# Three matrix loads of the expert loop, each cut into transfers of 112, 8 and 8 partitions

## The chip, the cores and the metric

The kernel runs on one core of one Trainium2 chip. The metric is the device time of one execution in microseconds (us). Three runs of the kernel before gave 1307.75, 1304.37 and 1307.27 us, so the median is 1307.27 us. All arithmetic is in float32.

## The reference, cut to what matters

One inference step of a one-layer decoder for 256 prompt tokens and 32 sample tokens (8 requests of 4 tokens): RWKV-7 time mixing and a convolution module side by side, cross-attention over memory tokens, then a mixture of 32 experts of which each token takes 4. The change touches only the mixture of experts:

```python
for e in range(N_EXPERTS):                       # 32 experts, D_MODEL = D_EXPERT = 1024
    gate = jnp.minimum(t @ w_gate[e] + b_gate[e], SWIGLU_LIMIT)
    up = jnp.clip(t @ w_up[e] + b_up[e], -SWIGLU_LIMIT, SWIGLU_LIMIT)
    hid = (up + 1.0) * gate * jax.nn.sigmoid(gate * SWIGLU_ALPHA)
    y = y + comb[:, e:e + 1] * (hid @ w_down[e] + b_down[e]).astype(jnp.float32)
```

Each expert has three matrices of 1024 x 1024 float32, which is 4 MB each. All 96 matrices are read from HBM once, some 403 MB.

## The kernel before, in words

The first 340 us or so compute the mixing, the convolution and the attention. The rest is the expert loop: 16 pairs of experts, numbered 0 to 15. For each pair TensorE multiplies by six matrices in this order: first gate, first up, second gate, second up, first down, second down (`MATRICES`). Each product is 32 matmuls of `L1182`. Between them stand the transposes of the hidden rows (`L1199`, `L1207`), the gathering of the next pair's token rows (`L1211`), the bias rows (`L1193`) and the addition of the last pair's result to the output (`L1244`, `L1256`).

The matrices wait in ten slots of SBUF, each 128 partitions of 16 KB, six in the tensor `ring` and four in `arena`. In pairs 2 to 14 (`WHOLE`) a matrix goes as one transfer into two neighbouring slots: 128 rows of 32 KB, one row to each partition (`L465`). So five matrices fit at a time. In pairs 0, 1 and 15 a matrix goes as two halves of 2 MB or as smaller pieces (`L487`, `L485`, `L481`).

All these loads are issued by SyncE in program order. Before a load, SyncE waits (`wait_used`) until TensorE has finished the product that read what was in the slots, which is the matrix five places earlier. The load then stands in the DMA queue behind those issued before it. When a load has landed it adds 16 to the semaphore of its slot (`slot_in[i]`), and TensorE waits before the first matmul of a product until the semaphore stands at 16 times the number of loads that the slot has had (`landings`, used in `product`).

Ahead of pair 0's second gate matrix, `small()` (`L441`) loads three bias tables of 128 KB: each is 32 rows of 4 KB, to partitions 0 to 31, 32 to 63 and 64 to 95.

Of the kernel before, what the change touches and what calls it, by code (L numbers as in the profile page):

```python
# [21 lines left out]
P = 128  # L22
# [14 lines left out]
SLOTS = 10  # L37
TURN = (2, 3, 4, 5, 6, 7, 8, 9, 0, 1)
WHOLE = range(2, PAIRS - 1)
BIASED = 6  # L40
RING = 6
RW = 14
CT = 4
# [36 lines left out]
LOADS = 12 * PAIRS  # L80


def load_of(q, n, c):

    return 12 * q + 2 * n + c


def slot_of(load):

    return TURN[load % SLOTS]  # L90


def asked(load):

    return load | 1 if load // 12 in WHOLE else load


def landings(load):

    i = slot_of(load)  # L100
    return len({asked(l) for l in range(load + 1) if slot_of(asked(l)) == i})


PER_ROUND = [len({asked(l) for l in range(LOADS) if slot_of(asked(l)) == i}) for i in range(SLOTS)]
OPENED = 6


# [42 lines left out]
def build(nc, A, O):  # L150
    with ExitStack() as ctx:
        def sb(name, shape, dt=F32):
            return ctx.enter_context(nc.sbuf_tensor(name, shape, dt))

        def sem(name):
            return ctx.enter_context(nc.semaphore(name))

        def part(base, at, *dims):

            n = 1  # L160
            for d in dims:
                n *= d
            a = base[:, at:at + n]
            names = "abcd"[:len(dims)]
            if len(dims) == 1:
                return a
            return a.rearrange(f"p ({' '.join(names)}) -> p {' '.join(names)}", **dict(zip(names, dims)))

        SLOT = 4 * D
        SPARE = 27096 - (SLOTS - 8) * SLOT  # L170
        ring = sb("ring", [P, RING * SLOT])
        scratch = ring[:, 2 * SLOT:]
# [3 lines left out]
        vec = sb("vec", [P, VECW])  # L176
        slot = [part(ring, i * SLOT, KT, 512) for i in range(RING)]

        def weights(i):

            if i < RING:
                return ring[:, i * SLOT:(i + 1) * SLOT]
            at = (i - RING) * SLOT if i < 8 else SPARE + (i - 8) * SLOT
            return arena[:, at:at + SLOT]

        def whole_slot(i):

            if i < RING:
                return ring[:, (i - 1) * SLOT:(i + 1) * SLOT]
            at = 0 if i < 8 else SPARE  # L190
            return arena[:, at:at + 2 * SLOT]
# [89 lines left out]
        load = const[:, 1221:1222]  # L281
# [71 lines left out]
        slot_in = [sem(f"slot_in{i}") for i in range(SLOTS)]  # L353
# [26 lines left out]
        def _(sp):  # L380
# [58 lines left out]
            def small():  # L439
                for dst, name in ((b_gate, "b_gate"), (b_up, "b_up"), (b_down, "b_down")):  # L440
                    sp.dma_start(dst, A[name]).then_inc(S["ext_ld"], 16)  # L441
# [7 lines left out]
            def wait_used(r, load):  # L449

                q, n, c = load // 12, load % 12 // 2, load % 2
                if frees(n, c):
                    sp.wait_ge(S["used"], r * (USED * PAIRS) + used_up_to(load))
                else:
                    sp.wait_ge(S["up_done" if n in (1, 3) else "down_done"], r * (2 * PAIRS) + (2 * q + 1 + (n in (3, 5))))

            def experts(r, q):
                opening, last = isinstance(r, int) and q == 0, q == PAIRS - 1
                for n, (w, p) in enumerate(MATRICES):
                    e = 2 * q + p  # L460
                    if q in WHOLE:
                        load = load_of(q, n, 1)
                        i = slot_of(load)
                        wait_used(r, load - SLOTS)
                        sp.dma_start(whole_slot(i), w[e, :, :]).then_inc(slot_in[i], 16)  # L465
                        continue
                    for c in range(2):
                        load = load_of(q, n, c)
                        i = slot_of(load)
                        src = w[e, :, c * SLOT:(c + 1) * SLOT]  # L470
                        if load < SLOTS:
                            if opening and i < len(last_front):
                                name, val = last_front[i]
                                sp.wait_ge(S[name], val)
                        elif not (opening and n == 5):
                            wait_used(r, load - SLOTS)
                        if opening and i == RING:
                            small()
                        if last and n == 5:
                            for k in range(4):  # L480
                                sp.dma_start(weights(i)[:, k * D:(k + 1) * D], src[:, k * D:(k + 1) * D]).then_inc(S[LAST_ROWS[c][k]] if k < 3 else slot_in[i], 16)  # L481
                        elif opening and n == 5:
                            for k in range(4):
                                sp.wait_ge(S["used"], 4 * c + k + 1)
                                sp.dma_start(weights(i)[:, k * D:(k + 1) * D], src[:, k * D:(k + 1) * D]).then_inc(S["x_in"] if k < 3 else slot_in[i], 16)  # L485
                        else:
                            sp.dma_start(weights(i), src).then_inc(slot_in[i], 16)  # L487
# [9 lines left out]
            for q in range(PAIRS):  # L497
                experts(0, q)
# [4 lines left out]
            with sp.Fori(1, ROUNDS) as r:  # L503
                with sp.If(n > r * CAP):
                    for q in range(PAIRS):
                        experts(r, q)
                    final_rows(r)
                    results(r)
                    sp.wait_ge(S["out_sent"], r * (16 * PARTS) + 16 * PARTS)
                    sp.sem_inc(S["router_in"], 1)  # L510
# [85 lines left out]
        def _(pe):  # L596
# [569 lines left out]
            def product(out, lhs, r, q, n, ks, fresh, done=None, swap=False):  # L1166

                opening, pieces, whole = isinstance(r, int) and q == 0, q == PAIRS - 1 and n == 5, q in WHOLE
                for k in ks:
                    load = load_of(q, n, k // 4)  # L1170
                    i = slot_of(load)
                    if pieces and k % 4 < 3:
                        pe.wait_ge(S[LAST_ROWS[k // 4][k % 4]], r * 16 + (48 if k == 2 else 32))
                    elif whole and k == 0 or not whole and k % 4 == 0 or pieces and k % 4 == 3:
                        come = slot_of(asked(load))
                        pe.wait_ge(slot_in[come], r * (16 * PER_ROUND[come]) + 16 * (FRONT_FILLS[come] + landings(asked(load))))
                    if opening and n == 0 and k == 4:
                        pe.wait_ge(S["xe_ready"], 2)
                    if opening and n == 5 and k == 0:
                        pe.wait_ge(S["x_in"], 16 + 6 * 16)  # L1180
                    for h in range(2):
                        last = nc.tensor.matmul(out[AT[h ^ swap], :], lhs(k), part(weights(i), 0, 4, D)[:, k % 4, h * 512:(h + 1) * 512],  # L1182
                                                start=(fresh and k == 0), stop=(k == KT - 1), skip_group_check=True)
                    if opening and n == 0 or k % 4 == 3 and frees(n, k // 4):
                        last.then_inc(S["used"], 1)
                if done and k == KT - 1:
                    last.then_inc(S[done], 1)
# [74 lines left out]
            def step(r, q, s):  # L1262
# [11 lines left out]
                opening = isinstance(s, int) and first  # L1274
                biased = isinstance(s, int) and q == BIASED
                half, rest = range(KT // 2), range(KT // 2, KT)
# [949 lines left out]
```

## Time and profile before

| | |
|---|---|
| median of 3 runs | 1307.27 us |
| the profiled execution | 1306.09 us |
| its span, first to last instruction | 1304.3 us |
| TensorE busy | 1265.9 us (97%) |
| VectorE, ScalarE busy | 412.6 us, 192.3 us |
| moved by DMA | 464.67 MB, 356 GB/s over the span |
| granted TensorE clock, mean | 0.993 |

The span is the time between the first and the last instruction of the profiled execution; 1.8 us of the execution lie outside it. A busy TensorE is read from modelled ends of matmuls. The DMA share of a stretch is the part of it in which the core's 16 DMA engines, on average, had a packet under way: 1.00 is all sixteen all the time. GB/s is what arrived meanwhile. The two together tell whether the engines are idle or slow.

### The profile page before, as it was taken

What the parts mean: (1) busy time and instruction counts of PE and PEld (TensorE: products, weight loads), DVE (VectorE), ACT (ScalarE), POOL (GpSimd) and SP (SyncE); (2) the same over time, 40 slices, a digit from 0 to 9 for tenths busy, and PEclk for the clock granted to TensorE, in tenths of its full rate; (3) what the DMA queues carried; (4) which work ended last, traced back from release to release, by engine and by line L of the source; (5) the groups of instructions that cost most, each with busy time, mean ns of one, the idle gap of its engine ahead of it and who ended that gap; (6) DMA issues with size and microseconds to landing.
All of it is one profiled execution on the core that took longest, in us unless ns stands there. A gap on an engine that the chain in (4) does not pass through costs nothing.

```text
span 1304.3 us, 18542 instructions
## 1 busy us (share of the span) xinstructions
PE 1265.9 (97%) x8160; PEld 623.3 (48%) x8160; DVE 412.6 (32%) x836; ACT 192.3 (15%) x353; POOL 11.7 (1%) x31
## 2 busy tenths in 40 slices
PE   9999999999999999999999999999999999999995
PEld 7777865677763443434434343443334343343332
DVE  4987745433122122131222212122121212212122
ACT  4114322221121010000100000010000001010002
POOL 0001000000000000000000000000000000000000
PEclk9999999999999999999999999999999999999998
DMA  9333041495999999999999999999999999999993
GB/s 319 131 107 141 4 140 60 164 379 227 414 409 426 427 433 432 433 428 432 432 431 431 428 431 433 433 433 426 430 431 433 434 431 431 428 430 433 425 424 143
DMA packets 30335, 464.67 MB, mean 356 GB/s; under 512 B 7329, under 2 KB 8865, under 8 KB 12465
## 3 DMA queue, kind: packets, MB, share of 16 engines
q1 hardware_dynamic: 29600, 459.53, 83.9%
q0 software_dynamic: 656, 3.96, 0.7%
q8 instruction: 66, 1.08, 0.3%
q14 instruction: 13, 0.10, 0.0%
HBM read 458.34 MB, written 5.14 MB: 355 GB/s over the span
## 4 chain that ended last, share of the span: by engine, by line
PE 78%; DMA 18%; DVE 1%; ACT 1%; issue 0%; SPq 0%; DVEq 0%
PE ps L1182 39%; PE ps L605 25%; DMA ring<-in_w_down 9%; DMA arena<-in_w_down 9%; PE ps L1211 5%; PE ps L1256 3%; PE ps L1193 2%; PE ps L1207 1%; PE ps L1199 1%; PE ps L1304 1%; DVE ring L1602 0%; DMA ring<-in_w_in 0%; PE ps L1244 0%; PE ps L1258 0%; DVE arena L1605 0%
## 5 line engine op out<-in xcount | busy, mean ns | idle before, releaser
L1182 PE MATMUL ps<-ring,xT 128*64 128x512 f32 x1216 | 270.8, 595 | 0.7 <-DMA ring<-in_w_up 0.6
L605 PE MATMUL ps<-arena,ring 128*128 128x288 f32 (+3 forms) x1136 | 225.4, 366 | 1.4 <-DMA ring<-in_w_in 1.3
L605 PEld LDWEIGHTS ps<-arena,ring 128*128 128x128 f32 (+1 forms) x1136 | 176.7, 177 | 47.7 <-issue 4.7
L1182 PE MATMUL ps<-arena,xT 128*64 128x512 f32 x832 | 185.5, 595 | 0.1
L1357 ACT ACTIVATE arena<-ps 128x512 f32<-128x512 f32 (+5 forms) x136 | 76.4, 570 | 630.2 <-PE ps L1199 363.2
L1182 PEld LDWEIGHTS ps<-ring,xT 128*64 128x64 f32 x1216 | 83.9, 137 | 176.6 <-issue 173.2
L1182 PE MATMUL ps<-ring,arena 128*64 128x512 f32 x640 | 145.1, 601 | 8.0 <-DMA ring<-in_w_down 8.0
L1182 PEld LDWEIGHTS ps<-arena,xT 128*64 128x64 f32 x832 | 57.4, 137 | 120.3 <-issue 117.6
L1182 PE MATMUL ps<-arena 128*64 128x512 f32 x384 | 87.6, 604 | 7.6 <-DMA arena<-in_w_down 7.6
L1182 PEld LDWEIGHTS ps<-ring,arena 128*64 128x64 f32 x640 | 45.2, 138 | 92.7 <-issue 91.6
L2065 DVE TENSOR_TENSOR arena<-arena,ps 128x512 f32<-128x512 f32 x64 | 44.0, 687 | 130.2 <-PE ps L1256 117.3
L2017 DVE TENSOR_TENSOR xT<-ps,vec 128x1024 f32<-128x1024 f32 x15 | 18.4, 1224 | 173.6 <-PE ps L1211 173.6
L1256 PE MATMUL ps<-arena 128*128 128x512 f32 x128 | 63.8, 619 | 0.0
L1211 PE MATMUL ps<-arena 128*128 128x128 f32 x512 | 62.8, 282 | 0.0
L1211 PEld LDWEIGHTS ps<-arena 128*128 128x128 f32 x512 | 59.8, 196 | 2.0 <-issue 0.2
L2075 DVE TENSOR_SCALAR xT<-ps 128x512 f32<-128x512 f32 x32 | 22.1, 691 | 121.1 <-PE ps L1193 121.1
L605 PE MATMUL ps<-ring,arena 128*32 128x256 f32 (+4 forms) x456 | 59.1, 382 | 0.8 <-ACT arena L1357 0.8
L1182 PEld LDWEIGHTS ps<-arena 128*64 128x64 f32 x384 | 27.2, 139 | 58.6 <-issue 57.9
L1551 ACT ACTIVATE xT<-xT 128x512 f32<-128x512 f32 x32 | 20.1, 630 | 237.1 <-DVE xT L2075 237.1
L1605 DVE SCALAR_TENSOR_TENSOR arena<-arena,vec 128x256 f32<-128x256 f32 x128 | 51.5, 481 | 2.5 <-ACT arena L1370 2.5
L2080 DVE TENSOR_SCALAR xT<-ps 128x512 f32<-128x512 f32 x32 | 22.0, 687 | 81.7 <-PE ps L1182 81.7
L2105 DVE COPY arena<-ps 64x512 f32<-64x512 f32 x16 | 10.9, 683 | 99.3 <-PE ps L1182 99.3
(227 smaller groups left out, 765.6 us busy)
## 6 DMA issues: line engine op xcount, KB each, us to landing
ring<-in_w_gate SPq DMA_DIRECT2D x16, 4096.0 KB, 34.8
ring<-in_w_up SPq DMA_DIRECT2D x16, 4096.0 KB, 35.1
ring<-in_w_down SPq DMA_DIRECT2D x14, 4096.0 KB, 36.9
arena<-in_w_down SPq DMA_DIRECT2D x12, 4096.0 KB, 35.0
arena<-in_w_gate SPq DMA_DIRECT2D x10, 4096.0 KB, 32.6
arena<-in_w_up SPq DMA_DIRECT2D x10, 4096.0 KB, 35.4
ring<-in_w_down SPq DMA_DIRECT2D x8, 2048.0 KB, 19.7
ring<-in_w_gate SPq DMA_DIRECT2D x6, 2048.0 KB, 17.6
```

The source lines that it names most:

```text
L605: return nc.tensor.matmul(out, lhsT, rhs, start=start, stop=stop)
L1182: last = nc.tensor.matmul(out[AT[h ^ swap], :], lhs(k), part(weights(i), 0, 4, D)[:, k % 4, h * 512:(h + 1) * 512], start=(fresh and k == ...
L1193: last = nc.tensor.matmul(out[AT[h], :], one_e[o, p, :], b[:, h * 512:(h + 1) * 512], start=(out is psU), stop=(out is psG), skip_group_ch ...
L1211: last = nc.tensor.matmul(to[:, k * P:(k + 1) * P], h_tok[:, j, k * P:(k + 1) * P], pick[:, j, :, :], start=False, stop=(j == 1), skip_gro ...
L1256: last = nc.tensor.matmul(out, gT[:, h, j * P:(j + 1) * P], ye[h], start=True, stop=not biased, skip_group_check=True)
L1357: return a.activation(out, in_, ACT.Copy, scale=scale)
L1551: nc.scalar.activation(sig, gmin, ACT.Sigmoid, scale=1.702).then_inc(S["sig_ready"], 1)
L1605: return v.scalar_tensor_tensor(out, x, s, y, o0, o1)
L2017: nc.vector.tensor_tensor(xe.rearrange("p k a c -> p k (a c)"), psX.rearrange("p (k t) -> p k t", k=KT), g_moe.unsqueeze(2).broadcast_to([ ...
L2065: nc.vector.tensor_tensor(y[:, j, at], y[:, j, at], (psY, psX)[j][:, at], ALU.add).then_inc(S["y_added"], 1)
L2075: nc.vector.tensor_scalar(gmin, psG, 7.0, None, ALU.min).then_inc(S["g_ready"], 1)
L2080: link(nc.vector.tensor_scalar(ug, psU, 7.0, -7.0, ALU.min, ALU.max))
```

## The change

The first gate matrix of pairs 3, 7 and 11 is no longer one transfer of 128 partitions but three, issued one behind the other: partitions 0 to 111, 112 to 119 and 120 to 127. They go to the same two slots, read the same rows of HBM and add to the same semaphore, 48 in place of 16. Loads are now counted by transfers, so that TensorE's wait for this product and for later ones of that slot ask for the higher count. Nothing else is computed or loaded otherwise.

```diff
+UNEVEN = (3, 7, 11)
+SHARES = (slice(0, 112), slice(112, 120), slice(120, 128))
...
+def shares(load):
+
+    return SHARES if load // 12 in UNEVEN and load % 12 < 2 else (slice(0, P),)
+
+
+def transfers(i, loads):
+
+    return sum(len(shares(load)) for load in {asked(l) for l in loads} if slot_of(load) == i)
+
+
 def landings(load):
 
-    i = slot_of(load)
-    return len({asked(l) for l in range(load + 1) if slot_of(asked(l)) == i})
-
-
-PER_ROUND = [len({asked(l) for l in range(LOADS) if slot_of(asked(l)) == i}) for i in range(SLOTS)]
+    return transfers(slot_of(load), range(load + 1))
+
+
+PER_ROUND = [transfers(i, range(LOADS)) for i in range(SLOTS)]
...
-                        sp.dma_start(whole_slot(i), w[e, :, :]).then_inc(slot_in[i], 16)
+                        for rows in shares(load):
+                            sp.dma_start(whole_slot(i)[rows], w[e, rows, :]).then_inc(slot_in[i], 16)
```

SyncE's queue before, from the last loads of pair 2 to the first of pair 3:

```order
L465 DMA ring<-in_w_down 128x8192 [waits down_done]
L453 REGISTER_ALU
L465 DMA arena<-in_w_down 128x8192 [waits used]
L455 REGISTER_ALU
L465 DMA arena<-in_w_gate 128x8192 [waits up_done]
L453 REGISTER_ALU
L465 DMA ring<-in_w_up 128x8192 [waits used]
L455 REGISTER_ALU
L465 DMA ring<-in_w_gate 128x8192 [waits up_done]
```

The same place now:

```order
L477 DMA ring<-in_w_down 128x8192 [waits down_done]
L464 REGISTER_ALU
L477 DMA arena<-in_w_down 128x8192 [waits used]
L466 REGISTER_ALU
L477 DMA arena<-in_w_gate 112x8192 [waits up_done]
L477 DMA arena<-in_w_gate 8x8192 x2
L464 REGISTER_ALU
L477 DMA ring<-in_w_up 128x8192 [waits used]
L466 REGISTER_ALU
L477 DMA ring<-in_w_gate 128x8192 [waits up_done]
```

The load of the first gate matrix is 112 partitions wide and is followed by two of 8 partitions, with no wait of their own; everything else keeps its place. Pairs 7 and 11 change in the same way. On TensorE, VectorE, ScalarE and GpSimd no operation is added, removed or moved; only numbers that TensorE and SyncE wait for are others.

## Rows read from the trace of the kernel before

**Rows 1.** The page: engines' busy time, DMA share by slices, instruction fetches.
```profile
PE 1265.9 (97%) x8160; PEld 623.3 (48%) x8160; DVE 412.6 (32%) x836; ACT 192.3 (15%) x353; POOL 11.7 (1%) x31
...
DMA  9333041495999999999999999999999999999993
...
q8 instruction: 66, 1.08, 0.3%
```

**Rows 2.** Windows, pairs 2 to 14: busy us, clock, DMA share, GB/s.
```profile
core 0: us, PE busy (x) PEld busy (x) DVE busy (x) ACT busy (x) POOL busy (x), PEclk, DMA share, GB/s
455.00:1215.00 760.00, 743.70 (x3819) 284.83 (x3817) 169.25 (x314) 65.34 (x107) 0.00 (x0) 1.00 1.00 431
```

**Rows 3.** DMA queues, same stretch: packets, MB, share of 16 engines.
```profile
q1 hardware_dynamic: 11270, 326.98, 100.1%
q8 instruction: 30, 0.49, 0.3%
```

**Rows 4.** Who TensorE waited for: us in total, times, longest.
```profile
PE ps L1182 <- DMA ring<-in_w_down: 8.0, 3, 2.7
PE ps L1182 <- DMA arena<-in_w_down: 7.6, 3, 2.7
...
PEld ps L1182 <- DMA ring<-in_w_up: 3.3, 3, 1.5
PEld ps L1182 <- DMA arena<-in_w_up: 2.7, 3, 0.9
```

**Rows 5.** Chain of waits, pairs 9 to 10: start us, us, what.
```profile
883.79 38.19 DMA arena<-in_w_down
...
922.12 3.65 PE ps L1182 x16
...
941.86 38.41 DMA ring<-in_w_down
...
980.40 3.65 PE ps L1182 x16
```

**Rows 6.** Chain of waits, pair 14 to the end.
```profile
1176.55 38.40 DMA arena<-in_w_down
...
1215.09 5.03 PE ps L1182 x16
...
1275.93 10.48 PE ps L1182 x47
```

**Rows 7.** Windows at the end of the last weight load.
```profile
1274.00:1276.00 2.00, 2.00 (x14) 0.73 (x12) 0.17 (x1) 0.04 (x1) 0.00 (x0) 1.00 1.02 401
1276.00:1278.00 2.00, 2.00 (x10) 0.63 (x10) 0.00 (x0) 1.97 (x3) 0.00 (x0) 1.00 0.63 231
1278.00:1280.00 2.00, 2.00 (x12) 0.72 (x10) 0.00 (x0) 0.52 (x2) 0.00 (x0) 1.00 0.51 209
...
1282.00:1284.00 2.00, 2.00 (x12) 0.64 (x10) 0.00 (x0) 0.00 (x0) 0.00 (x0) 1.00 0.49 195
```

**Rows 8.** Windows around the landing of the bias tables.
```profile
354.00:356.00 2.00, 2.00 (x10) 1.58 (x9) 0.46 (x1) 0.11 (x1) 0.00 (x0) 1.00 1.02 434
356.00:358.00 2.00, 2.00 (x14) 0.99 (x14) 0.45 (x1) 0.44 (x1) 0.00 (x0) 1.00 1.13 275
358.00:360.00 2.00, 2.00 (x10) 1.56 (x9) 0.46 (x1) 0.00 (x0) 0.00 (x0) 1.00 0.95 256
360.00:362.00 2.00, 2.00 (x10) 1.54 (x9) 0.24 (x1) 0.00 (x0) 0.00 (x0) 1.00 1.03 330
362.00:364.00 2.00, 2.00 (x10) 1.58 (x9) 0.67 (x2) 0.44 (x1) 0.00 (x0) 1.00 0.96 410
```

**Rows 9.** DMA issues between 334 and 336 us: KB, us to landing.
```profile
arena<-in_b_gate SPq DMA_DIRECT2D x1, 128.0 KB, 24.1
...
arena<-in_b_down SPq DMA_DIRECT2D x1, 128.0 KB, 27.3
```

**Rows 10.** Windows while 512 KB pieces of 128 partitions land (4 KB rows).
```profile
391.00:397.00 6.00, 6.00 (x48) 2.50 (x42) 0.94 (x3) 2.30 (x3) 0.00 (x0) 1.00 1.02 408
```

**Rows 11.** Timeline of SyncE's queue, then of TensorE, around pair 3's first gate matrix.
```profile
509.45 0.33 SPq L465 DMA_DIRECT2D arena<-in_w_gate  x1
519.77 0.33 SPq L465 DMA_DIRECT2D ring<-in_w_up  x1
...
547.08 7.04 PE L1182 MATMUL ps<-arena,xT 128*64 128x512 f32 x32
```

## The prediction

> **What bounds the kernel now.** I read the page first. TensorE is busy for 1265.9 us, 97% of the span, and the DMA engines are busy in every slice from about a quarter of the span on [rows 1]. Two resources are nearly full, so the averages don't tell which one sets the end.
>
> The windows do. Over pairs 2 to 14 the DMA share is 1.00 and 431 GB/s arrive, while TensorE is idle for 760 - 743.7 = 16.3 us [rows 2]. A matrix of 4.19 MB takes 4.19 MB / 431 GB/s = 9.73 us, and six take 58.4 us. The chain of waits shows the same period: the wait that ends at 922.12 us comes again at 980.40, 58.3 us later [rows 5]. TensorE needs less for a pair: 58.3 less the 2.7 us that it waited for a down matrix and some tenths for an up matrix, about 55 us. So the DMA engines are the slower of the two throughout. In the early pairs this doesn't show, because the five slots hold matrices ahead; the gate matrix that is issued at 509.45 us is only needed at 547.08, 37.6 us later [rows 11]. From pair 9 on the stock is used up, and TensorE waits six times for a down matrix, 15.6 us together, and 6.0 us for up matrices [rows 4]. What the queues lose before that is not forgiven: since they never rest, a loss at pair 3 is still there at pair 10.
>
> The last such wait ends at 1215.09 us [rows 6]. From there TensorE runs almost without a gap to the end, so the kernel's end moves with the landing of pair 14's first down matrix, one for one.
>
> The third view is the end of the stream. Up to 1276 us all sixteen engines work; from 1278 to 1284 the share is 0.51 to 0.49 and about 209 GB/s arrive [rows 7]. Eight engines had finished and eight were still at it, 8 us late. A load has landed only when its last engine has, so TensorE always waits for the late eight. Why they are late: there were 66 instruction fetches, 0.3% of sixteen engines' 1304 us [rows 1], which is 0.003 x 16 x 1304 = 63 us. If they all fall on eight engines, that is 7.8 us for each, and the 8 us are explained.
>
> **The change part by part.** *Rows moved.* The queue moved 326.98 MB in 11270 packets, 29 KB each with the few small ones [rows 3], so a 32 KB row goes as one packet on one engine, and an engine takes 9.73 / 8 = 1.22 us for it. 112 rows are 7 for each of 16 engines. Eight rows can be spread over eight engines at most, and if both small transfers use the same eight, these get 9 rows and the others 7. Three times this is 3.65 us more for one half and 3.65 us less for the other. If the early half gets the extra rows, it ends at 1276 + 3.65 = 1279.7 and the late half at 1284 - 3.65 = 1280.3: nearly even. With nothing else, the end comes 3.65 us earlier.
>
> No row shows which engines a small transfer takes. The Trainium skill ("DMA: Bandwidth & Descriptors", Why a DMA increments its semaphore by 16 and not by 1) says that a transfer uses the largest number up to 16 that divides its slowest dimension, and on this queue the lowest-numbered engines: 16 for 112 rows, the first eight for 8 rows.
>
> *Issues.* Six more DMA issues at 0.33 us each [rows 11] are 2.0 us of SyncE, at places where it has 8 to 10 us until its next wait ends (509.45 to 519.77). They cost nothing while the queue holds matrices, and at most 0.7 us a place if it didn't. TensorE's waits are the same in number.
>
> *Narrow targets.* This term decides. The trace has narrow transfers at one place: three bias tables of 32 partitions, 393 KB together, that land between 358 and 363 us (issued between 334 and 336, 24.1 to 27.3 us to landing) [rows 9]. There the rate falls from 434 to 275, 256, 330 and 410 GB/s while the DMA share stays about 1 [rows 8]. The engines were not idle; their packets took longer. Against 431 GB/s this is (156 + 175 + 101 + 21) x 2 us = 906 KB not moved, 2.1 us of the whole stream. It isn't the small rows: pieces of the same 4 KB rows, but over 128 partitions, go at 408 GB/s [rows 10], which would cost 0.1 us here. So writes that aim at few partitions hold each other up, and others' too.
>
> The new transfers aim at 8 partitions, 262 KB each. Bounds for the two of one matrix, 524 KB: nothing, if eight engines on eight partitions don't meet; at the bias tables' price per byte 2.1 x 524 / 393 = 2.8 us. If the price grows as the target narrows, 32 / 8 = four times this, 11.2 us. The dear end: sixteen engines fill 128 partitions at 431 GB/s, 26.9 GB/s for 8 partitions; if 8 neighbours have no more than that, the two transfers take 19.5 us in place of 2 x 1.22, 17.1 us more. I take 9.7 us: it is between 2.8 and 17.1 and near the scaled value, which is the only one that uses both the measured loss and the width. It falls on the eight engines that carry the small transfers.
>
> The skill states a rule that speaks against the change ("SBUF — State Buffer", Door 1: The DMA port swizzle): SBUF has 16 DMA ports of 27.2 GB/s, and groups of four neighbouring partitions share one, so 8 neighbours reach two ports. It gives 27.6 GB/s measured on partitions 0 to 3. By it the two small transfers take 2 x 262 KB / 54.4 GB/s = 9.6 us, an estimate, and 12 us with the other half's own rows on these ports; that is 7.2 to 9.6 us over the free price. The trace agrees in kind [rows 8] and has no 8-partition write to measure.
>
> *Sum.* The half with the small transfers loses 1.22 + 9.7 = 10.9 us a matrix, 32.8 us over three. It was 8.0 us ahead, so the last landing comes 24.8 us later. The other half gains 3.65 us, which helps nothing. Nothing hides the loss: the stock of five slots was going to be empty at pair 9 anyway, and now is empty some pairs sooner. 1306.09 + 24.8 = 1330.9 us. The profiled run is 1.2 us below the median of the three, within their spread, so I say 1331.
>
> **The rivals.** *Balance.* The narrow writes cost nothing, and the late half does less: 1306.1 - 3.65 = 1302.4 us, or 1303.6 against the median. For it: eight engines are late by 8 us [rows 7], and 3.65 us each way meets that closely. Against it: rows 8. It decides if the narrow term is below (8.0 - 3.65) / 3 = 1.4 us a matrix.
>
> *Light price.* The bias price per byte, 2.8 us for every engine or 5.6 us on one half: 3 x (1.22 + 2.8 or 5.6) - 8.0 = 4.1 to 12.5 us, 1310 to 1319. For it: it is the measured figure as it stands.
>
> *The wide part collides too.* In one transfer of 128, eight rows belong to each engine and nothing collides (431 GB/s). Seven rows for each may put several engines on the same partitions' path. If that holds up half to all of their 8.5 us, another 4.3 to 8.5 us a matrix, 13 to 26 us: 1344 to 1357. No row shows a transfer of 112.
>
> *Wrong half.* The extra rows go to the engines that are already late: with no narrow price 1306.1 + 3.65 = 1309.7, with it 1306.1 + 32.8 = 1339. The rows can't tell the halves apart.
>
> *Nothing.* If the small transfers are spread over all engines after all, the time stays at 1306 to 1307.
>
> **How the numbers follow.** Forecast, narrow price near 9.7 us, 1322 to 1340: 0.52. Balance 0.17. Light price 0.10. Wide part collides 0.14. Wrong half without a narrow price 0.04. Nothing 0.03. The range of 1302 to 1346 holds balance, and leaves out most of the dear case. This kernel's measurement tells 0.3% from no change, 3.9 us. Balance lies just at this bound, so half of it, 0.09, counts as faster; its other half with nothing and a third of the wrong half, 0.12, as the same; the rest, 0.79, as slower.
>
> **What would show it.** Right: in windows of 2 us after about 525, 760 and 1000 us GB/s falls well below 400 for 8 to 15 us while the DMA share stays near 1; the mean over pairs 2 to 14 falls from 431 to about 417 GB/s; TensorE's first wait for a down matrix comes two to four pairs sooner, and its waits for DMA grow from 21.6 to about 46 us; the gate loads' time to landing grows. Balance: no dips, the windows after 1276 us fall from full share to nothing within 2 us, and the waits shrink by 3.65 us. Light price: dips as at 356 us and no deeper. A dip that begins with the 112-row part is the third rival. I am wrong if no dip stands at these three places.

## The result, and the profile after

The changed kernel takes 1369.43 us (median of 6 runs, 1363.79 to 1374.04); the kernel before took 1305.53 us in the same comparison. The ratio is 1.0484, 95% interval 1.0456 to 1.0512: 63 us slower, give or take 4. The forecast was slower by 24.8 us, 1331, with a range up to 1346. The direction was right and the size was not. The profile below is of the execution that took 1363.79 us, the fastest of the six and 57.7 us above the profiled one of before.

The page of the changed kernel, its engines and its DMA by slices:

```profile
span 1362.0 us, 18548 instructions
...
PE 1280.5 (94%) x8160; PEld 629.4 (46%) x8160; DVE 412.8 (30%) x836; ACT 192.2 (14%) x353; POOL 11.7 (1%) x31
...
DMA  8342052478999999999999999999999999999993
GB/s 307 124 152 86 3 187 98 172 295 356 403 410 429 433 429 255 432 429 432 430 430 432 309 332 430 429 431 431 431 383 209 424 431 433 431 431 430 427 418 115
```

The DMA share is as full as in [rows 1], but three dips stand in GB/s: 255, then 309 and 332, then 383 and 209. They are where the cut matrices of pairs 3, 7 and 11 land. Between them the rate is the 431 GB/s of [rows 2]. The windows of the changed kernel (columns as in [rows 2]), first the whole stretch, then the three dips, then the first dip in two parts:

```profile
455.00:1240.00 785.00, 726.53 (x3668) 279.78 (x3666) 159.08 (x295) 62.83 (x103) 0.00 (x0) 0.97 1.00 402
520.00:550.00 30.00, 30.00 (x172) 12.67 (x168) 6.58 (x14) 3.00 (x5) 0.00 (x0) 1.00 0.98 243
765.00:800.00 35.00, 17.66 (x98) 9.00 (x98) 2.11 (x4) 2.30 (x4) 0.00 (x0) 0.77 1.00 226
1010.00:1065.00 55.00, 30.55 (x142) 12.96 (x140) 4.19 (x7) 2.37 (x4) 0.00 (x0) 0.78 1.00 259
...
500.00:516.00 16.00, 16.00 (x76) 4.99 (x72) 5.86 (x9) 0.63 (x1) 0.00 (x0) 1.00 1.01 435
518.00:532.00 14.00, 14.00 (x70) 4.43 (x68) 4.46 (x10) 1.04 (x2) 0.00 (x0) 1.00 0.98 234
532.00:542.00 10.00, 10.00 (x74) 6.29 (x72) 0.16 (x1) 1.78 (x3) 0.00 (x0) 1.00 1.03 144
545.00:560.00 15.00, 15.00 (x74) 4.71 (x72) 3.37 (x7) 0.61 (x2) 0.00 (x0) 1.00 0.99 425
```

Time lost in a stretch is its length times the missing share of 431 GB/s. Over the whole stretch that is 785 x (1 - 402/431) = 52.8 us. The dips give 30 x (1 - 243/431) = 13.1, 16.6 and 22.0 us, 51.7 together: the whole loss is in them, and it grows from one to the next. (The first dip begins 2 us ahead of its window, which adds 0.9 us.) In the first dip the 112-row part comes first, 14 us at 234 GB/s, a loss of 6.4 us; then come the 8-row parts, 10 us at 144 GB/s, a loss of 6.7 us.

The DMA queue of the changed kernel at 480 to 510 us, where nothing is cut, then in the two parts of the first dip (packets, MB, share of 16 engines):

```profile
q1 hardware_dynamic: 442, 12.91, 100.0%
q1 hardware_dynamic: 109, 3.28, 98.4%
q1 hardware_dynamic: 72, 1.44, 103.1%
```

A packet is one row of 32 KB, apart from those of 4 bytes. By the MB these are 394 rows, then 100, then 44, and they share the time of sixteen engines: 1.22 us a row, then 2.2, then 3.75. The packets' own records say that no engine was spared. From 518 to 531.5 us no row took less than 1.69 us, and from 534 to 540 none of 27 less than 3.63. At least 11 of the 27 belong to other transfers, since the two small ones have 16 rows in all.

Who TensorE waited for in the changed kernel (total us, times, longest), to be read beside [rows 4]:

```profile
PE ps L1194 <- DMA ring<-in_w_down: 19.2, 7, 7.0
PE ps L1194 <- DMA ring<-in_w_gate: 15.7, 2, 14.5
PE ps L1194 <- DMA arena<-in_w_gate: 14.4, 1, 14.4
PE ps L1194 <- DMA arena<-in_w_down: 10.0, 5, 2.7
```

59.3 us in place of 15.6, with two waits of over 14 us. The 14.4 us are a wait for a cut matrix, the first gate matrix of pair 7: the timeline has its end in the third row. In the course of the wait the granted clock falls from 1.00 to 0.50, and it stays there for the first 5 us or so of the work behind it (0.77 and 0.78 in the dips' means).

```profile
769.50 3.84 PE L1223 MATMUL ps<-arena 128*128 128x128 f32 x32
776.23 8.78 PE L1194 MATMUL ps<-ring,arena 128*64 128x512 f32 x32 [2.90 <-DMA ring<-in_w_down]
799.46 2.83 PE L1194 MATMUL ps<-arena,xT 128*64 128x512 f32 x6 [14.44 <-DMA arena<-in_w_gate]
```

With 5.6 us for which the weight loads of TensorE's array (PEld) waited, its waits for DMA are 65 us, where the forecast had about 46. The first wait for a down matrix ends at 642 us, in pair 4, five pairs sooner than before.

The end of the stream, which answers to [rows 7]:

```profile
1334.00:1336.00 2.00, 2.00 (x10) 0.57 (x8) 0.00 (x0) 1.97 (x3) 0.00 (x0) 1.00 0.28 100
...
1338.00:1340.00 2.00, 2.00 (x12) 0.71 (x10) 0.00 (x0) 0.69 (x2) 0.00 (x0) 1.00 0.13 52
...
1342.00:1344.00 2.00, 2.00 (x12) 0.48 (x8) 0.00 (x0) 0.00 (x0) 0.00 (x0) 1.00 0.06 25
```

Before, eight engines were late together. Now the stage at half share is gone: up to 1334 us the share is about 0.9, then 0.13 is two engines and 0.06 is one. So the two halves came out level, and one or two engines straggle for another 10 us. Before, eight engines ended at 1276 us and eight at 1284, 1280 in the mean. Most now end at 1334, 54 us later, but the last is done at 1344, 60 us later, and a load has landed only when its last engine is done.

### The profile page after: what moved, and what is told of

Same layout as the page of the kernel before. It is cut to its first block, busy times and chain, and to the rows that moved or that the text cites. A ratio compares the mean times of both kernels' runs of the same rounds, so it can differ in the third digit from the quotient of the medians.

```text
span 1362.0 us, 18548 instructions
## 1 busy us (share of the span) xinstructions
PE 1280.5 (94%) x8160; PEld 629.4 (46%) x8160; DVE 412.8 (30%) x836; ACT 192.2 (14%) x353; POOL 11.7 (1%) x31
## 4 chain that ended last, share of the span: by engine, by line
PE 67%; DMA 26%; another core or an unknown queue 3%; DVE 1%; ACT 1%; issue 0%; SPq 0%; DVEq 0%
PE ps L1194 32%; PE ps L617 24%; DMA arena<-in_w_down 14%; DMA ring<-in_w_down 12%; PE ps L1223 4%; PE ps L1268 2%; PE ps L1219 1%; PE ps L1205 1%; PE ps L1211 1%; DVE ring L1614 0%; DMA ring<-in_w_in 0%; PE ps L1316 0%; PE ps L1256 0%; DVE arena L1617 0%
## 5 line engine op out<-in xcount | busy, mean ns | idle before, releaser
L1194 PE MATMUL ps<-ring,xT 128*64 128x512 f32 x1216 | 273.0, 599 | 15.9 <-DMA ring<-in_w_gate 15.7
L1194 PE MATMUL ps<-arena,xT 128*64 128x512 f32 x832 | 187.9, 602 | 14.6 <-DMA arena<-in_w_gate 14.4
L1194 PE MATMUL ps<-ring,arena 128*64 128x512 f32 x640 | 150.2, 619 | 19.2 <-DMA ring<-in_w_down 19.2
L1563 ACT ACTIVATE xT<-xT 128x512 f32<-128x512 f32 x32 | 20.1, 630 | 272.3 <-DVE xT L2087 272.3
L2070 DVE TENSOR_TENSOR arena<-arena,ps 128x256 f32<-128x256 f32 x16 | 6.7, 422 | 135.2 <-PE ps L1256 128.1
```

The source lines that it names most:

```text
L1563: nc.scalar.activation(sig, gmin, ACT.Sigmoid, scale=1.702).then_inc(S["sig_ready"], 1)
```

## The experiments

Theories: **P**, the path theory: groups of partitions are each reached by one path, as wide as one DMA engine, and engines that aim at one path at the same time share it, in the 112-row part too. **N**: only narrow pieces cost, the forecast. **S**: small transfers cost by themselves. Further rivals stand in the expectations. Each kernel is the changed one with other `UNEVEN` or `SHARES`, unless it says otherwise. Changes of time are (ratio - 1) x 1305.5 us.

**Two transfers, 112 and 16 partitions.**

```diff
-SHARES = (slice(0, 112), slice(112, 120), slice(120, 128))
+SHARES = (slice(0, 112), slice(112, 128))
```

> First gate matrix of pairs 3, 7 and 11 as two transfers, 112 and 16 partitions, so that every engine again gets eight rows. Theory N (my forecast: only the narrow piece costs, and more the narrower it is): the piece is twice as wide and on sixteen engines, price at most half of 11 us a matrix, so +5 to +17 us against the kernel before. Theory P (groups of neighbouring partitions share a path as wide as one engine; whenever several engines aim at the same group at once all of them slow down, the 112-row part included): the 112 rows still collide, so +30 to +50 us, and the dip in GB/s starts with the 112-row part. Theory S (small transfers on few engines cost by themselves): no more than +3 us.

Measured: ratio 1.0370 (1.0344 to 1.0396), +48 us. Three quarters of the loss are still there. N allowed 17 us and S 3, and both fall; P's range holds. The windows of this kernel, the 112-row part of pair 3 and then the 16-row part:

```profile
524.00:536.00 12.00, 12.00 (x60) 3.71 (x58) 3.65 (x9) 0.63 (x1) 0.00 (x0) 1.00 1.03 254
537.00:546.00 9.00, 9.00 (x67) 5.38 (x64) 0.00 (x0) 1.78 (x3) 0.00 (x0) 1.00 1.02 175
```

The dip begins with the 112-row part, as P had said. By these windows the wide part loses 12 x (1 - 254/431) = 4.9 us and the 16-row part 5.3, so the +48 us aren't the wide part's alone.

**Two halves of 64 partitions.**

```diff
+SHARES = (slice(0, 64), slice(64, 128))
```

> The same three matrices as two transfers of 64 partitions, four rows for each engine. Theory P: if the 64 partitions of a half are served by half of the paths, each transfer runs at half rate and takes 9.7 us in place of 4.9, +9.7 us a matrix, +29 us in all, with GB/s near 215 while they land; somewhat less where early engines are already at the other half. Theory N: 64 partitions are wide, less than +5 us. Theory S: 0.

Measured: 1.0331 (1.0297 to 1.0365), +43 us. Ahead of the cut matrix, and while it lands:

```profile
500.00:515.00 15.00, 15.00 (x70) 4.68 (x68) 3.68 (x6) 0.63 (x1) 0.00 (x0) 1.00 1.00 429
520.00:540.00 20.00, 20.00 (x110) 7.20 (x107) 4.46 (x10) 2.41 (x4) 0.00 (x0) 1.00 0.99 206
```

206 GB/s is half of 429, which is what P said of 64 neighbours on half of the paths. The loss is 14 us a matrix and not 9.7: the slow stretch is longer, 26 us (518 to 544) in place of the two transfers' own 19.5.

**Three transfers cut by columns.** Control: each over all 128 partitions.

```diff
+SHARES = ((slice(0, P), slice(0, 4 * D)), (slice(0, P), slice(4 * D, 6 * D)), (slice(0, P), slice(6 * D, 8 * D)))
...
+                        for rows, cols in shares(load):
+                            sp.dma_start(whole_slot(i)[rows, cols], w[e, rows, cols]).then_inc(slot_in[i], 16)
```

> The same three matrices as three transfers again, but cut by columns (16, 8 and 8 KB of every row), each over all 128 partitions. Theory P: no two engines aim at one path, nothing is lost: -1 to +1 us. Theory S (three transfers in place of one, shorter packets): up to +3 us a matrix.

Measured: 1.0000 (0.9985 to 1.0016). The stretch in which pair 3's cut matrix lands:

```profile
515.00:545.00 30.00, 30.00 (x174) 13.19 (x172) 7.46 (x14) 3.66 (x6) 0.00 (x0) 1.00 1.00 425
```

Cutting a load in three costs nothing, so S falls here too. The loss comes from which partitions go together in a transfer.

**Sixteen neighbours, or sixteen that lie apart** (pair 7 alone).

```diff
+UNEVEN = (7,)
+SHARES = tuple(slice(16 * k, 16 * k + 16) for k in range(8))   # neighbours
+SHARES = tuple(slice(k, k + 121, 8) for k in range(8))         # apart
```

> Only pair 7's first gate matrix is cut: eight transfers of 16 neighbouring partitions, one 32 KB row for each of the 16 engines in each. Theory P (paths of four neighbours plus the four that lie 32 away, each as wide as one engine; packets of one path share it): 16 neighbours reach four paths, four packets share one, a packet takes 4 x 1.21 = 4.9 us, the matrix 39 us in place of 9.7: +29 us. Theory W (only the number of partitions in a transfer counts, not which): some loss, but the same as for 16 partitions that lie apart.

> As the kernel with 16 neighbours, with every eighth partition in each transfer (0, 8, ..., 120 and so on): same number of transfers, rows, engines and bytes. Theory P: eight paths, two packets share one, 2.4 us a packet, 19.4 us for the matrix: +10 us, about a third of the neighbours' loss. Theory W: as with 16 neighbours.

Measured: neighbours 1.0157 (1.0135 to 1.0179), +20.5 us; apart 1.0120 (1.0105 to 1.0135), +15.7 us. The intervals touch, but the windows are far apart. Each figure is off P's, +29 and +10. Neighbours, then apart, while the matrix lands:

```profile
758.00:784.00 26.00, 17.50 (x108) 8.58 (x104) 2.39 (x5) 2.37 (x4) 0.00 (x0) 0.92 0.99 159
```

```profile
758.00:776.00 18.00, 16.63 (x104) 8.30 (x100) 2.11 (x4) 2.37 (x4) 0.00 (x0) 1.00 0.98 207
```

Same rows, engines and number of transfers, and 159 against 207 GB/s: the place counts, as P says and W denies. Over the whole of 755 to 800 us the rates are 234 and 303 GB/s, losses of 20.6 and 13.4 us, which is 7 us apart like the medians of the two kernels (1327.68 and 1320.75 us). 207 is near the half rate of two to a path. 159 is more than P's quarter (108). A reason that fits, but wasn't tested: an engine goes on to the next transfer without waiting for the others, so several transfers, and their paths, are under way at once.

**Eight neighbours, or eight that lie apart, in short pieces.** The matrix goes as 28 KB of every row for 128 partitions, then 16 transfers of 8 partitions with the last 4 KB.

```diff
+SHARES = ((slice(0, P), slice(0, 7 * D)),) + tuple((slice(8 * k, 8 * k + 8), slice(7 * D, 8 * D)) for k in range(16))
...
+SHARES = ((slice(0, P), slice(0, 7 * D)),) + tuple((slice(32 * g + j, 32 * g + j + 29, 4), slice(7 * D, 8 * D))
+                                                   for g in range(4) for j in range(4))
...
```

> The same three matrices: 7 of 8 KB-columns groups (28 KB of each row) for all 128 partitions in one transfer, and the last 4 KB of every row in 16 transfers of 8 neighbouring partitions. As in the changed kernel one row's worth moves to the engines of the small transfers, and nothing is 112 wide. Theory N and theory P agree in sign: eight engines aim at eight neighbours each time; P puts it at 16 x 0.61 us in place of 16 x 0.15 for these engines, +7.3 us a matrix and +1.2 for the row moved, 25.5 us less the lead of 8.0: +17 us. N: as the changed kernel's narrow part, +25 us. Theory S: -3.65 to +3 us.

> As the kernel with 16 transfers of 8 neighbouring partitions, but each of the 16 transfers takes every fourth partition of a block of 32 (0, 4, ..., 28 and so on): same bytes, same number of transfers, same engines, only the partitions of one transfer lie apart. Theory P: no two engines of one transfer meet; only where the small transfers write partitions that the other eight engines also write do they share. +0 to +5 us, 12 us or more below the kernel with neighbours. If moving a row from the late to the early half helps by itself: -3.65 us. Theory S and N (width 8 counts, not place): as the kernel with neighbours.

Measured: neighbours 1.0087 (1.0055 to 1.0119), +11.4 us; apart 1.0101 (1.0074 to 1.0127), +13.2 us. No difference, and P had said 12 us or more. No theory gave either figure: P had 17 and 0 to 5, N 25 for both, S at most 3. The windows of the short pieces of pair 3, neighbours and then apart, agree too:

```profile
526.00:534.00 8.00, 8.00 (x42) 2.74 (x40) 2.08 (x3) 0.44 (x1) 0.00 (x0) 1.00 1.03 292
```

```profile
528.00:536.00 8.00, 8.00 (x40) 2.77 (x38) 2.08 (x3) 0.60 (x1) 0.00 (x0) 1.00 1.03 285
```

This speaks against P as it stands. A reason that would save it, but was only argued: over all sixteen pieces each path gets the same bytes in both, and the eight engines that carry them are free to drift over several pieces; what is left in both is that these engines write to the other eight engines' paths. What the runs do show is that this way of moving one row's worth to another half of the engines, which has no 112-row part and in the second form no two rows of one piece in the same group of four partitions, still costs 4 us a matrix where balance promised a gain.

**One cut matrix alone.**

```diff
+UNEVEN = (3,)     # and (5,), (11,), (13,)
```

> The changed kernel with pair 3 alone cut into 112, 8 and 8. Its dip lasts some 26 us at 243 GB/s, a loss of 13 to 15 us. Theory A (the losses add up, each lasts to the end): +13 to +16 us. Theory B (the three losses of 14, 20 and 25 us grow because each leaves the engines further apart for the next): the same here, and pair 11 alone costs no more than pair 3 alone. Theory C (they grow because of what is different at pair 11, where TensorE is starved already and the target lies in the other tensor): pair 11 alone costs over 20 us.

> The changed kernel with pair 11 alone cut into 112, 8 and 8. Pair 3 alone cost 16.2 us; all three cost 64, which is 15 more than three times that. Theory B (each loss leaves the engines further apart for the next): pair 11 alone costs 13 to 18 us. Theory C (the place matters: the engines are already 8 us apart there, TensorE has no stock left, and the target is the other tensor): 21 to 27 us.

> The changed kernel with pair 5 alone cut. Pair 3 alone (target in arena, engines some 4 us apart, stock full) cost 16.2 us, pair 11 alone (target in ring, 7 us apart, no stock) 24.5. Pair 5's matrix goes to ring, with the engines about 4.5 us apart and the stock not yet used up. Theory T (the target tensor matters): 22 to 26 us. Theory L (the distance between early and late engines matters, since over that time the cut matrix also collides with its neighbours in the queue) and theory K (the empty stock matters): 15 to 19 us.

> Pair 13 alone cut: target in arena, engines 8 us apart, no stock. Theory T: as pair 3, about 16 us. Theories L and K: 24 to 28 us; L says more than pair 11's 24.5, K the same.

| cut | ratio | us | target | TensorE's stock |
|---|---|---|---|---|
| pair 3 | 1.0128 (1.0111 to 1.0145) | +16.7 | arena | full |
| pair 5 | 1.0147 (1.0126 to 1.0168) | +19.2 | ring | not used up |
| pair 11 | 1.0185 (1.0157 to 1.0212) | +24.2 | ring | empty |
| pair 13 | 1.0154 (1.0131 to 1.0176) | +20.1 | arena | empty |

(The 14, 20 and 25 us in the first expectation were read from the landing times of matrices ahead and behind; the windows above give 13.1, 16.6 and 22.0.) The windows of the landing at pair 3 and at pair 11, each in its own kernel:

```profile
518.00:544.00 26.00, 26.00 (x154) 11.76 (x154) 5.56 (x11) 3.66 (x6) 0.00 (x0) 1.00 1.03 197
```

```profile
984.00:1024.00 40.00, 20.59 (x110) 9.65 (x106) 2.11 (x4) 2.37 (x4) 0.00 (x0) 0.77 1.00 208
```

The rate is nearly the same, 197 and 208 GB/s, and at pair 11 it lasts 40 us in place of 26. In pair 3's kernel the time of a row falls from over 4 us to 1.3 within some 3 us (541 to 544, medians). In pair 11's it stays at 2.2 to 2.6 us for another 10 us behind the slowest rows (1010 to 1020).

Theory B falls, since pair 11 costs more without any cut before it. T is outside both new intervals: pair 5 should have cost 22 us or more and has 16.5 to 21.9, pair 13 about 16 and has 17.1 to 23.0. L and K have pair 5 within theirs, but both wanted 24 us or more at pair 13. Pair 13 is 4 us below pair 11, and these two intervals overlap, so neither the empty stock nor the distance between early and late engines is excluded as a part of the cause. Why the slow stretch is longer later on stays open. The losses do seem to add up: 63 us less pair 3's 16.7 and pair 11's 24.2 leaves 22 for pair 7, which no run cut alone in this way.

**Bias tables on 128 partitions.** The kernel before, with its one narrow place mended.

```diff
-                for dst, name in ((b_gate, "b_gate"), (b_up, "b_up"), (b_down, "b_down")):
-                    sp.dma_start(dst, A[name]).then_inc(S["ext_ld"], 16)
+                sp.dma_start(arena[:, 13056:14080], A["b_all"]).then_inc(S["ext_ld"], 16)
...
```

> The kernel before, with its three bias tables of 32 partitions each loaded as one transfer of 128 partitions (the fourth block of 32 is zeros, 131 KB more). Theory P: the stretch of 275, 256 and 330 GB/s at 356 to 362 us goes, 2.1 us of the stream come back, less 0.3 us for the added bytes: -1.8 us, which the clock hardly tells from nothing but the windows do: no stretch of 2 us between 350 and 370 us under 400 GB/s. If the dip had another cause (4 KB rows, the start of the expert loop): it stays.

Measured: 1.0002 (0.9991 to 1.0013). The windows answer to [rows 8]:

```profile
356.00:358.00 2.00, 2.00 (x10) 1.58 (x9) 0.69 (x2) 0.44 (x1) 0.00 (x0) 1.00 1.08 459
358.00:360.00 2.00, 2.00 (x15) 1.05 (x13) 0.34 (x1) 0.00 (x0) 0.00 (x0) 1.00 0.86 358
360.00:362.00 2.00, 2.00 (x12) 1.53 (x9) 0.57 (x2) 0.44 (x1) 0.00 (x0) 1.00 1.07 446
362.00:364.00 2.00, 2.00 (x10) 1.58 (x9) 0.00 (x0) 0.00 (x0) 0.00 (x0) 1.00 1.02 432
```

The mean over 8 us is 424 GB/s where it was 318, so 8 x 106 / 431 = 2.0 us of the stream came back; one window is at 358, below the 400 that was expected. The dip did come from the narrow target: the rows are of 4 KB as before, and the number of transfers alone cost nothing with the columns cut. The kernel's time gained nothing that shows. Its interval is -1.2 to +1.7 us and just leaves out the 1.8 us that were expected, so where these 2.0 us went is open.

## Why the prediction was wrong

**What bounds the kernel** held. The DMA queues never rest, and nothing hid the loss: 52.8 us are missing in the windows, and the execution they are from is 57.7 us longer. The 5 us between these two fit the stragglers at the end of the stream, though no run tested it. The other 5 us to the median's 63 lie in slower executions, of which there is no trace.

**Issues at nothing** held: three transfers in place of one cost 0.0% with the columns cut.

**The signs.** Dips stand at the three places with the DMA share near 1, as forecast. They are deeper: the mean over pairs 2 to 14 fell to 402 GB/s, not to 417. The first dip begins with the 112-row part, which the prediction had named as the sign of its third rival.

**The sign and the kind of the narrow term** held. The Trainium skill ("SBUF — State Buffer", Door 1: The DMA port swizzle) gives 64 neighbouring partitions eight of sixteen ports, an asymptote of 218 GB/s; measured 206, so the trace agrees for 64. The 8-row parts run at 144 GB/s, other rows included.

**The term that failed: the 112-row part was priced at nothing.** The sum took seven rows at 1.22 us each for an engine's share of it; they took 2.2 us each. Its extra cost was left out, and the collision of this part stood among the rivals with 0.14. It loses 6.4 us in the first dip, about as much as the 8-row parts' 6.7. With a 16-row piece in place of the two of 8, +48 of the +63 us remain. The prediction's own sentence, that in one transfer of 128 "eight rows belong to each engine and nothing collides", points at a reason: with seven rows an engine's rows may no longer match the paths. That much is P's account; no trace here names the rows of an engine.

**Who pays, and the 8 us of lead.** The sum put the narrow loss on the eight engines with small transfers and let their lead of 8.0 us pay for part. But sharing slows both sides: in the narrow part too no row took less than 3.63 us, on whichever engine. The loss is 13.1 us of the whole stream at the first matrix, where the sum had 10.9 us for half of the engines. By the sum the early half would have ended 28 us behind the other (1308.8 and 1280.3 us); it came out level with it. Using up the lead brought the last landing 4 us closer to the mean at most (1284 and 1280 us before), and the stragglers took more than that back. Three times 13.1 is 39 us already.

**Three equal losses** failed as well: 13.1, 16.6, 22.0. One matrix alone costs 17 to 24 us by its place. This makes up most of the rest, and its cause is open.

**The rival "balance".** The rows that led to it are real, eight engines 8 us late [rows 7], though that instruction fetches made them so was never tested. Where rows were moved, the halves did come out level. The stage at half share is gone in the three kernels with 8-row transfers at three matrices (here, and with sixteen pieces, neighbours or apart), and it is still there with the columns cut (0.53, 0.51), with 112 and 16 rows (0.61, 0.51) and with 64 and 64 (0.59, 0.56). What failed is that the narrow writes were to cost nothing. In no kernel here did moving rows bring a gain. That it could never do so was not shown: a narrow transfer that costs nothing wasn't found.

**The rival "wide part collides"**, 1344 to 1357, had the wide part's loss and was still 12 us short at its upper end: it kept the narrow loss on half of the engines, the whole 8 us of lead, and three equal losses. That the time would grow was forecast, but the sum had less than half of the growth.

## What to carry to other kernels

When a load is cut, cut it by columns, so that every piece spans all 128 partitions; that was free here, while pieces of 112, 64, 16 or 8 partitions ran at a third to two thirds of the rate while they landed. A DMA share of 1.00 says only that packets are under way, so read GB/s beside it. And before pricing the odd piece of a split, price the big one: it had changed its shape too.

## What the runs showed of the hardware that I had not expected

A transfer of 112 partitions runs at 234 to 254 GB/s against 431 for 128 partitions, with all sixteen engines at work (share 0.98 and 1.03). What is lost isn't lost by the narrow transfer alone: rows of other transfers in flight took three times as long (3.6 to 4.7 us in place of 1.22). Sixteen transfers of eight neighbours and sixteen of eight partitions four apart, in 4 KB pieces, cost the same (292 and 285 GB/s while they land), though with 32 KB rows and sixteen partitions the place did matter (159 and 207 GB/s). And after a long wait TensorE's clock was low: the engine stood still from 785.0 to 799.5 us; the granted clock was 1.00 up to 786, 0.79 from 786 to 788, 0.50 (1.2 GHz) from 788 to 804, 0.94 from 804 to 806 and 1.00 again (2.4 GHz) behind that.
